# Remainders in single passes, probabilities scaled by the product that turns them, and fourteen selection rounds in the softmax stage of a two-layer decoder step

## The reference, cut to what matters

```python
# A: sparse attention, 6 heads on 2 key heads, dim 64
score = einsum(relu(q_idx . k_idx), w)            # indexer, causal
_, sel = lax.top_k(score, 128)                    # each query keeps 128 keys
attn = softmax(where(selected and causal, q.k / 8, -inf))
o = attn @ v
# B: stick-breaking attention, 6 heads, dim 64, strictly causal
z = q.k / 8
log_rem = where(strict, log_sigmoid(-z), 0)
rev = cumsum(log_rem, reverse=True)               # over the keys
a = exp(where(strict, z + rev, -inf));  o = a @ v
```

## Time and profile before

| | |
|---|---|
| median of 3 runs | 1605.23 us |
| profiled execution, its own time | 1604.69 us |
| its span | 1602.9 us |
| mean granted TensorE clock | 0.989 |
| PE busy | 1544.2 us, 96% |
| DVE busy | 871.3 us, 54% |
| ACT busy | 683.5 us, 43% |
| DMA | 140.24 MB, mean 87 GB/s |

### The profile page before, as it was taken

One profiled execution on the slowest core, in us unless ns is written; L12 is line 12 of the kernel. 1 busy time (PEld: TensorE's weight loads), 2 busy tenths in 40 slices (PEclk: granted clock), 3 DMA queues, 4 the chain that ended last, 5 costly groups with the idle time before them and its releaser, 6 DMA issues.

```text
span 1602.9 us, 30655 instructions
## 1 busy us (share of the span) xinstructions
PE 1544.2 (96%) x11764; PEld 1407.4 (88%) x11772; DVE 871.3 (54%) x1564; ACT 683.5 (43%) x995; POOL 265.5 (17%) x466
## 2 busy tenths in 40 slices
PE   6999989999999999999999998899999999999998
PEld 5787745999999999999978775579999999999997
DVE  6568883345555553223857788624455555522345
ACT  4445455344444442224444445634544444322241
POOL 4120340111111110000123106102111111101000
PEclk8999999999999999999999999999999999999999
DMA  4233044223222223222223312333223323333221
GB/s 144 91 105 94 27 138 111 59 74 92 88 87 86 87 80 110 86 86 80 80 70 110 107 40 75 105 82 93 80 82 89 91 83 89 98 88 91 83 77 61
DMA packets 225719, 140.24 MB, mean 87 GB/s; under 512 B 13122, under 2 KB 219604, under 8 KB 225552
## 3 DMA queue, kind: packets, MB, share of 16 engines
q1 hardware_dynamic: 223220, 133.46, 28.9%
q0 software_dynamic: 2400, 5.42, 1.1%
HBM read 131.21 MB, written 7.65 MB: 87 GB/s over the span
## 4 chain that ended last, share of the span: by engine, by line
PE 81%; DVE 12%; issue 3%; ACT 3%; SPq 0%; DMA 0%; DVEq 0%; POOL 0%; ACTq 0%; POOLq 0%
PE ps L1728 24%; PE ps L1730 23%; PE ps L1729 23%; DVE score L1393 3%; DVE m L1390 3%; DVE w_L L1278 1%; PE ps L2084 1%; DVE aL L1290 1%; PE ps L2013 1%; PE ps L1755 1%; DVE Lb L1465 1%; PE ps L1812 1%; PE ps L1924 1%; PE ps L2168 1%; DVE stat L1512 1%
## 5 line engine op out<-in xcount | busy, mean ns | idle before, releaser
L1278 DVE TENSOR_TENSOR w_L<-w_raw,w_H 128x1024 fp32r<-128x1024 f32 (+4 forms) x236 | 256.8, 1097 | 421.0 <-ACT w_H L897 418.3
L1728 PE MATMUL ps<-bH,w_H 128*128 128x272 f32 x1664 | 481.0, 289 | 4.6 <-DVE w_L L1278 3.2
L1730 PE MATMUL ps<-bH,w_L 128*128 128x272 f32 x1664 | 479.5, 288 | 0.0
L1729 PE MATMUL ps<-bL,w_H 128*128 128x272 f32 x1664 | 477.7, 287 | 0.0
L897 ACT ACTIVATE w_H<-w_raw 128x1024 fp32r<-128x1024 f32 (+4 forms) x236 | 220.2, 943 | 297.7 <-PE ps L1730 287.9
L1728 PEld LDWEIGHTS ps<-bH,w_H 128*128 128x128 f32 x1664 | 312.5, 188 | 6.3 <-DVE w_L L1278 4.1
L1729 PEld LDWEIGHTS ps<-bL,w_H 128*128 128x128 f32 x1664 | 313.5, 188 | 0.1
L1730 PEld LDWEIGHTS ps<-bH,w_L 128*128 128x128 f32 x1664 | 312.6, 188 | 0.0
L1728 PE MATMUL ps<-actH,w_H 128*128 128x272 f32 x704 | 204.2, 290 | 0.0
L1730 PE MATMUL ps<-actH,w_L 128*128 128x272 f32 x704 | 203.7, 289 | 0.0
L1729 PE MATMUL ps<-actL,w_H 128*128 128x272 f32 x704 | 202.7, 288 | 0.0
(11 more groups left out here) (351 smaller groups left out, 2333.2 us busy)
## 6 DMA issues: line engine op xcount, KB each, us to landing
w_raw<-in_w_up SPq DMA_DIRECT2D x88, 512.0 KB, 3.7
w_raw<-in_w_down SPq DMA_DIRECT2D x32, 512.0 KB, 3.8
w_raw<-in_w_in SPq DMA_DIRECT2D x24, 512.0 KB, 5.5
w_raw<-in_w_ple_gate SPq DMA_DIRECT2D x16, 512.0 KB, 3.9
w_raw<-in_w_down SPq DMA_DIRECT2D x16, 384.0 KB, 3.4
w_raw<-in_w_out SPq DMA_DIRECT2D x16, 320.0 KB, 3.5
w_raw<-in_w_in SPq DMA_DIRECT2D x8, 452.0 KB, 4.9
w_raw<-in_w_in SPq DMA_DIRECT2D x8, 384.0 KB, 3.4
```

The source lines that it names most:

```text
L1278: ins = dve.tensor_tensor(w_L[u % SPLIT][:, a:b], w_raw[raw_slot(l, u)][:, a:b], w_H[u % SPLIT][:, a:b].bitcast(F32), ALU.subtract)
L1728: pe.matmul(out, wh, xh, start=start, stop=False)
L1729: pe.matmul(out, wh, xl, start=False, stop=False)
L1730: return pe.matmul(out, wl, xh, start=False, stop=stop)
```

## The change

It has three parts. (1) Each head's logarithms are split into fp32r parts (L_high by an ACT copy, L_low by a DVE subtraction), the two constant matrices are copied to fp32r once a layer, and remainders runs single-pass products over both parts, triangles first. L_low lies in the memory of Lb, L_high in that of Ab. (2) a_norm no longer scales the probabilities; it scales the identity (128 columns) by the reciprocal, into diag (six buffers), and a_turn becomes a product of the probabilities with diag. (3) In DVE's order 14 rounds of select(3) now stand in the softmax stage, two after each u < 7, decode_queries after u = 7. With these, feature_out works by halves, with a semaphore f_mm for the first half of a feature, and in turns 0 and 1 PE puts feature(2q+4, 0) ahead of the remainders and b_out in the middle of the second half.

```diff
+                def stick_high(h):
+                    act.wait_ge(b_dve, at(b_dve, 4 * (h // 2) + h % 2 + 1))
                     if h >= 2:
                         act.wait_ge(b_o, at(b_o, h - 1))
+                    copy(L_high[:, h % 2, :], Lb[:, h % 2, :]).then_inc(b_act, 1)
                 def stick_weights(h):
                     act.wait_ge(b_tri, at(b_tri, h + 1))
                     act.activation(Ab[:, h % 2, :], bz_all(h), ACT.Exp).then_inc(b_exp, 1)
...
                     stick_ln(e1, r1)
-                    split(U_F + 2 * q + 5)
                     if q == 0:
                         act.wait_ge(ak_out, at(ak_out, 5 * 16))
                         act.wait_ge(ix_out, at(ix_out, 5 * 16))
+                    stick_high(e0)
+                    stick_high(e1)
+                    split(U_F + 2 * q + 5)
...
                 def feature_out(n):
-                    dve.wait_ge(w_used, at(w_used, U_F + n + SPLIT + 1))
+                    dve.wait_ge(f_mm, at(f_mm, n + 1))
                     if n < 6:
-                        dve.scalar_tensor_tensor(halves(featT[:, blk, :]), psh(b), 0.125 if n % 2 == 0 else 1.0,
-                                                 halves(r_all[:, :]), ALU.mult, ALU.mult).then_inc(f_ev, 1)
+                        for half in range(2):
+                            x = slice(HALF * half, HALF * half + HALF)
+                            if half:
+                                dve.wait_ge(w_used, at(w_used, U_F + n + SPLIT + 1))
+                            dve.scalar_tensor_tensor(featT[:, blk, x], ps[:, b + half, 0:HALF], 0.125 if n % 2 == 0 else 1.0,
+                                                     r_all[:, x], ALU.mult, ALU.mult).then_inc(f_ev, 1)
...
+                for i, m in enumerate((ntri, nones)):
+                    ins = dve.tensor_copy(con_r[:, P * i:P * i + P], m)
...
+                def stick_low(h):
+                    dve.wait_ge(b_act, at(b_act, 4 * (h // 2) + h % 2 + 3))
+                    lo(L_low[:, h % 2, :], Lb[:, h % 2, :], L_high[:, h % 2, :]).then_inc(b_dve, 1)
...
-                select(1, 6, 11)
+                select(1, 6, 10)
                 stick_max(0)
+                feature_out(3)
                 stick_max(1)
-                feature_out(3)
+                stick_low(0)
+                stick_low(1)
                 split(17)
-                select(1, 11, 16)
-                select(2, 0, 7)
+                select(1, 10, 16)
                 feature_out(4)
                 split(18)
-                select(2, 7, 10)
+                select(2, 0, 3)
                 stick_max(2)
+                feature_out(5)
                 stick_max(3)
-                feature_out(5)
+                stick_low(2)
+                stick_low(3)
                 split(19)
-                select(2, 10, 16)
-                select(3, 0, 4)
+                select(2, 3, 8)
                 feature_out(6)
                 split(20)
-                select(3, 4, 7)
+                select(2, 8, 11)
                 stick_max(4)
+                feature_out(7)
                 stick_max(5)
-                feature_out(7)
+                stick_low(4)
+                stick_low(5)
                 split(21)
...
-                select(3, 7, 13)
+                select(2, 11, 16)
+                select(3, 0, 2)
...
                     for n in range(2):
-                        pr = prob_of(u, n)[:, 0:P * (t + 1)]
-                        dve.tensor_scalar(pr, pr, stat[:, s, 3, n:n + 1], None, ALU.mult).then_inc(q_norm, 1)
+                        m = 2 * u + n
+                        if u >= 3:
+                            dve.wait_ge(pt_mm, at(pt_mm, m - SOFT + 1))
+                        dve.tensor_scalar(diag[:, m % SOFT, :], ident, stat[:, s, 3, n:n + 1], None, ALU.mult).then_inc(q_norm, 1)
...
-                    if u < 3:
-                        select(3, 13 + u, 14 + u)
-                    elif u == 4:
+                    if u < 7:
+                        select(3, 2 + 2 * u, 4 + 2 * u)
+                    elif u == 7:
                         decode_queries()
...
                 def remainders(h):
-                    pe.wait_ge(b_max, at(b_max, h + 1))
-                    for i in range(4):
-                        mm = pe.matmul(bz(h, i), ntri, b_blk(Lb, h, i), start=False, stop=i == 3, skip_group_check=True)
-                        for j in range(i + 1, 4):
-                            pe.matmul(bz(h, i, P * (j - i)), nones, b_blk(Lb, h, j), start=False, stop=j == 3, skip_group_check=True)
+                    pe.wait_ge(b_dve, at(b_dve, 4 * (h // 2) + h % 2 + 3))
+                    for part in (L_high, L_low):
+                        for i in range(4):
+                            mm = pe.matmul(bz(h, i), ntri_r, b_blk(part, h, i), start=False, stop=False, skip_group_check=True)
+                    for part in (L_high, L_low):
+                        for i in range(3):
+                            for j in range(i + 1, 4):
+                                mm = pe.matmul(bz(h, i, P * (j - i)), nones_r, b_blk(part, h, j), start=False,
+                                               stop=part is L_low and j == 3, skip_group_check=True)
                     mm.then_inc(b_tri, 1)
...
                     feature(2 * q + 3, 1)
+                    if q < 2:
+                        feature(2 * q + 4, 0)
                     remainders(2 * q)
                     if q < 2:
                         remainders(2 * q + 1)
-                        feature(2 * q + 4, 0)
+                        feature(2 * q + 4, 1, 0, 4)
                         b_out(q)
-                        feature(2 * q + 4, 1)
+                        feature(2 * q + 4, 1, 4, KD)
...
                     for b in range(m // 6 + 1):
-                        mm = pe.transpose(ps[:, TURN_BANK[m % 3], P * b:P * b + P], prob_of(m // 2, m % 2)[:, P * b:P * b + P], ident)
+                        mm = pe.matmul(ps[:, TURN_BANK[m % 3], P * b:P * b + P], prob_of(m // 2, m % 2)[:, P * b:P * b + P],
+                                       diag[:, m % SOFT, :], start=True, stop=True)
```

More of the change, by code:

```diff
@@ L165, in build @@
         r_col = sb("r_col", [P, TILES])
+        turn_scale = ExitStack()
+        sb("scale_skip", [P, (KD + 6) * T], F32, turn_scale)
+        diag = sb("diag", [P, 6, P], F32, turn_scale)
+        turn_scale.close()
         whole = ExitStack()
@@ L218, in build @@
         Ab = sb("Ab", [P, 2, LW], F32, stick)
+        stick.close()
+        stick = ExitStack()
+        L_low = sb("L_low", [P, 2, LW], F32R, stick)
+        L_high = sb("L_high", [P, 2, LW], F32R, stick)
+        stick.close()
+        stick = ExitStack()
+        sb("stick_skip", [P, 9896], F32, stick)
+        con_r = sb("con_r", [P, 2 * P], F32R, stick)
         stick.close()
@@ L363, in build @@
         ident = con[:, C_ID:C_ID + P]
+        ntri_r, nones_r = con_r[:, 0:P], con_r[:, P:2 * P]
         ntri, nones, mean = con[:, C_NTRI:C_NTRI + P], con[:, C_NONE:C_NONE + P], con[:, C_ONE:C_ONE + P]
@@ L1049, in stick_ln @@
                     act.wait_ge(act_step, steps.value(raised))
-                    act.activation(Lb[:, h % 2, :], Lb[:, h % 2, :], ACT.Ln, bias=one).then_inc(b_ln, 1)
+                    act.activation(Lb[:, h % 2, :], Lb[:, h % 2, :], ACT.Ln, bias=one).then_inc(b_act, 1)
+                def stick_high(h):
+                    act.wait_ge(b_dve, at(b_dve, 4 * (h // 2) + h % 2 + 1))
+                    if h >= 2:
+                        act.wait_ge(b_o, at(b_o, h - 1))
+                    copy(L_high[:, h % 2, :], Lb[:, h % 2, :]).then_inc(b_act, 1)
                 def stick_weights(h):
                     act.wait_ge(b_tri, at(b_tri, h + 1))
-                    if h >= 2:
-                        act.wait_ge(b_o, at(b_o, h - 1))
                     act.activation(Ab[:, h % 2, :], bz_all(h), ACT.Exp).then_inc(b_exp, 1)
@@ L1874, in feature @@
                             pe.wait_ge(p_ev, at(p_ev, 13 + half))
-                        elif n < 7:
-                            pe.wait_ge(f_ev, at(f_ev, n))
+                        elif n < 7 or half == 0:
+                            pe.wait_ge(f_ev, at(f_ev, 2 * n - 1 + (half or n == 3)))
                         else:
@@ L1883, in feature @@
                         mm = tri_product(ps[:, F_BANK[n] + half, 0:HALF], H[:, wk], Lo[:, wk], aH[:, k, x], aL[:, k, x], k == 0, k == KD - 1)
-                    if half and k1 == KD:
-                        mm.then_inc(w_used, 1)
+                    if k1 == KD:
+                        mm.then_inc(w_used if half else f_mm, 1)
                 for t in range(1, 4):
@@ L1899, in logits @@
                 def logits(q):
-                    pe.wait_ge(f_ev, at(f_ev, 2 * q + 2))
+                    pe.wait_ge(f_ev, at(f_ev, 4 * q + 4))
                     if q == 0:
@@ L1909, in logits @@
                         if q == 0 and i == 2:
```

(2 more changed lines are left out.)

11 lines of the change are left out of this document (6 added, 5 removed).

## The result

The changed kernel takes 1645.08 us (median of 4 runs, 1644.08 to 1646.12) beside 1605.36 us for the kernel before in the same session (1603.8 to 1611.15): ratio 1.0234, 95% interval 1.0211 to 1.0256. It is slower, by 40 us, where 29 were forecast; the profiled execution took 1646.12 us (span 1644.3), where the sum said 1633.5.

The account below looks back on a forecast made before the run. PE and DVE both bound the stick stage, with DVE's third selection deciding the logits of u = 9; 10.3 + 2.6 + 1.5 = 14.4 us a layer, 28.8 for two, on 1604.7 plus half a microsecond gave 1634 us, range 1620 to 1650.

Parts of the forecast that it names:

- the third selection must end before 227.7: Before the logits of u = 9: condition for the kernel getting faster, 1599 us; chance 0.05.
- the reserve of 9.2: Before the logits of u = 9: they started 9.2 us after the third selection ended; the change uses this up.
- DVE's line, 9.7 to the norm of u = 7: DVE from 125 us to the norm of u = 7: added less removed work and waits make it 9.7 us later.
- Low parts: DVE in the stick stage: six subtractions of 1280 columns a layer at 1.40 us each, 8.4 us.
- The new waits: DVE in the stick stage: it stands for features, ScalarE's cuts and logarithms, 4.4 us net of 0.8 already waited.
- Logits of u = 9, 10.3: PE in the softmax stage: these logits wait for the third selection and start some 10.3 us late.
- Doubled turns, 2.6: PE behind the logits of u = 9: 42 blocks at 0.23 us for 0.108, partly hidden in waits, net +2.6 us.
- The clock, 1.5 a layer: PE around the logits of u = 9: waiting lowers the granted clock, costing 1.5 us a layer (none to 4).
- Remainders: PE in the stick stage: a head's products fall from 4.3 to 2.7 us, saving 9.4 us a layer.
- rival (a): Remainders on PE: narrow fp32r products cost as much as fp32 ones, giving 1641 us; chance 0.20.
- The stick stage: PE's stick-breaking stage: gives back about 7.4 us a layer, 9.4 less the longer wait of the third turn.
- The wait of 4 us before head 4: PE in the third turn: the chain of maximum, high and low parts makes it wait some 4 us, 1.7 before.

Follow-up runs that it names:

- only_selection: The kernel before with the changed kernel's order of selection rounds and nothing else: 1643.51 us, ratio 1.0218.
- undo_remainders: The changed kernel with remainders as full fp32 products over the logarithms, no high or low part: 1650.39 us, ratio 1.0269.
- undo_turns: The changed kernel with probabilities scaled in place and turned by transposes as before: 1637.36 us, ratio 1.0187.
- paired_pool: The changed kernel with selection rounds interleaved in pairs, turns by transposes, and low parts of heads 0 to 3 subtracted by POOL: 1592.66 us, ratio 0.9895.

## Why the prediction was right, and its sizes

- **What bounds.** By the prediction "the third selection must end before 227.7", and with the reserve of 9.2 gone PE stands near 10 us for it. Right: 8.3 and 9.2 us in the change, 10.0 with the order alone (9.6 in its second layer).
- **DVE's line, 9.7 to the norm of u = 7.** It came 11.6 later (241.42 less 1.3, for 228.52). Low parts were 1.40 apart as priced in the first turn (two in 2.92), but the third pair took 3.95 with POOL's additions beside it, and a split 1.71 (175.16) for 1.22: some 1.6 us more than priced, beside POOL, for which the sum had no term. The new waits were 5.7 gross for 5.2. The first pairs of diagonals took 1.18 and 1.29 for 0.9.
- **What the prediction had wrong about that line.** It wrote that the rounds' "place does not matter for this sum" and gave 8.4 of its 9.7 to the low parts. The sum came near, but its largest term is not what the change costs: with no low parts at all the logits of u = 9 come 15.6 and 15.9 us late (only_selection), and undo_remainders, which takes them out, is 2.9 us later than the change. Where the low parts are gone DVE stands 14 us for features instead; where they are there it stands 5.7. 8.4 of low parts and 5.7 of standing make the same 14.1 us: the moved rounds opened that gap, and the low parts only fill it.
- **Logits of u = 9, 10.3.** 12.6 and 13.5. This follows from the line above; of layer 2's further 0.9 I did not find the place.
- **Doubled turns, 2.6.** 2.8 us with the clock up (26.8 for 24.0), as forecast. The price of 0.23 a block held: six take 1.34 us, 0.22 each, where a transpose took 0.108. The Trainium skill's rule (TensorE: Matmul & The Clock Gate, Terms), by which a transpose is four times as fast as an fp32 product, would by the prediction's figure have made 7.8 more of it (42 blocks at 0.43 for 0.23 are 8.4, so it was summed a little low); the rows show two times.
- **The clock, 1.5 a layer.** 2.0 to 2.9, up to twice the forecast: the granted clock was 0.64 and 0.51 from 228 to 248 us, so not only the logits of u = 9 (2.08 for 1.13 us) but the first turns behind them (2.70 for 1.34) ran slow. By the Trainium skill (TensorE: Matmul & The Clock Gate, Part 4: PE-mode transpose) transposes would not count as busy, and the prediction drew 0 for this term from it; the changed kernel, with products in place of transposes, fell to 0.51 all the same while PE waited. undo_turns, with transposes, kept 1.8 us of slow stretch (25.8 for 24.0; all of it between the logits of u = 9 and u = 10, 5.46 us for 3.69), about as much, so no run here shows a difference between the two kinds.
- **Remainders.** 2.8 us a head for the forecast 2.7; six products of 384, 256 and 128 columns take 0.75 us (139.80 to 140.55), so narrow fp32r products are not dear, and rival (a) falls. The stick stage gave back 4.9 and 5.6 us a layer, not 7.4: head 4 ran at the lower clock, 2.4 us too long, and nothing of it reached the total.
- **The wait of 4 us before head 4** was 3.92.
- **The total.** 14.4 a layer were 18.3. Up to the logits of u = 9 2.3 and 3.2 are short (DVE beside POOL, its waits, the diagonals), behind them 1.6 and 0.7 (the clock). Outside the layers' stretches lie 4.9 us on which the prediction had nothing. That 1645 is inside the range is in part luck: with its clock term at the dear end of 4 the forecast's own sum reaches 1639, and the range went to 1650 for rival (a), which fell.
- What the prediction did not see: that its own two causes overlap. Undoing one of them gives back little or nothing (1632 and 1650 us), and order alone is already the whole loss.

## What to carry to other kernels

An engine at 54% of the span can be the one that binds: add its own waits between dependent instructions to its busy time, then look for the appointment behind it. Work that is moved on such an engine counts twice: the place it leaves turns into idle time in front of a slot in the queue that comes too early, and the place it goes to has no cover. Before moving it, fill the engine's own waits with a second, independent chain; the two kernels here that did so without the split and the doubled turns (and with the rounds placed anew) stand 16 us below the kernel before, where the change stands 40 above it. The shorter products paid only behind that, and only once POOL had taken four of the six low parts and the wait before head 4 was shortened.

## What the runs showed of the hardware

- Dependent DVE instructions stand 0.15 us apart, independent ones overlap by 0.08: MAX8 of 256 columns, some 0.42 us long, is followed after 0.34 us by another MAX8 (141.59 to 141.93), and after 0.57 by the value load that needs it (130.85 to 131.42). The Trainium skill (VectorE: DVE Perf Modes, The DRAIN you can't avoid) says that leaving semaphores out between DVE operations saves nothing. No run here leaves one out; but what an instruction waits for does count: two rounds whose instructions each wait for the one just before take 2.68 us, the same work in two independent chains 1.71.
- DVE and POOL slow each other. DVE's subtraction of 1280 columns took 1.98 us each for 1.46 while POOL's addition of 496 columns took 2.56 for 1.26, in the changed kernel's third turn:

```profile
181.22 1.26 POOL L812 TENSOR_TENSOR pooled<-pooled,u_p 64x496 f32<-64x496 f32 x1 [0.18 <-POOL first L808]
...
185.39 2.56 POOL L812 TENSOR_TENSOR pooled<-pooled,u_p 64x496 f32<-64x496 f32 x1 [0.18 <-POOL first L808]
```

- POOL's subtraction of 1280 columns with an fp32r result takes 2.93 us, twice DVE's. Beside it DVE's MAX8 keep their 0.42 us (137.97 in paired_pool), but its own subtraction of 1024 columns takes 2.98 us (141.39) where others take 1.23. In these rows the operations with one tensor as input are untouched and those with two are slowed, which agrees with the Trainium skill (SBUF — State Buffer, Who interferes with whom). One input is no safeguard in every form, though: in the changed kernel two diagonals, a tensor times one value per row, took 1.18 and 1.29 us at 205.79 and 210.88, where POOL adds, and 0.48 from 221.18 on.
